# Three products of rounded halves for the projections outside the feed-forwards of a two-block transformer step

## What is computed

```python
def first_block(x, ...):
    h = rms_norm(x, norm_w)
    proj = h @ w_in            # 8200 columns: dn_qkv 1536, dn_z 512, b 4, a 4, swa_q/k/v 3 x 1536, swa_z 512, gates 2048
    qkv = silu(causal_depthwise_conv(dn_qkv, conv_w))
    o_dn = gated_delta_rule_chunked(l2(dq), l2(dk), dv, g, beta)      # chunks of 64, triangular solve
    y_dn = (rms_norm(o_dn, dn_norm_w) * silu(dn_z)) @ w_branch_dn
    ...                        # three dilated windows, 4 heads, rope, softmax over the groups
    y_swa = (o_swa * silu(swa_z)) @ w_branch_swa
    merged = sigmoid(g_dn) * y_dn + sigmoid(g_swa) * y_swa
    return x + merged @ w_out

def second_block(x, mem, ...):
    for l in range(2):
        x = x + 0.5 * swiglu(rms_norm(x, ffn1_norm), ffn1_w_in, ffn1_w_out)     # d_ff 2816
        z = rms_norm(x, mix_norm) @ w_mix_in                                     # 1696 columns
        o = concat(mla(z), swa(z), na(z)) with a norm of each group
        x = x + o @ w_mix_out
        x = x + mem_xattn(rms_norm(x, mem_norm_x), mem, ...)                     # 256 memory tokens, 4 heads of 64
        x = x + 0.5 * swiglu(rms_norm(x, ffn2_norm), ffn2_w_in, ffn2_w_out)
        x = rms_norm(x, block_norm)
    return x
```

## Time and profile before

| | |
|---|---|
| three runs, median (range) | 3507.95 us (3506.88 to 3508.4) |
| the profiled execution | 3507.39 us |
| its span in the profile | 3505.6 us |
| TensorE, matmuls busy | 3214.3 us, 92% |
| VectorE busy | 1275.5 us, 36% |
| ScalarE busy | 905.6 us, 26% |
| mean granted TensorE clock | 0.956 |
| DMA | 235.18 MB, 67 GB/s |

### The profile page before, as it was taken

One profiled execution on the slowest core, in us unless ns is written; L12 is line 12 of the kernel. 1 busy time (PEld: TensorE's weight loads), 2 busy tenths in 40 slices (PEclk: granted clock), 3 DMA queues, 4 the chain that ended last, 5 costly groups with the idle time before them and its releaser, 6 DMA issues. The chain is left out here.

```text
span 3505.6 us, 35266 instructions
## 1 busy us (share of the span) xinstructions
PE 3214.3 (92%) x12500; PEld 2167.7 (62%) x12500; DVE 1275.5 (36%) x1770; ACT 905.6 (26%) x1545; POOL 239.8 (7%) x184
## 2 busy tenths in 40 slices
PE   7978999989989999899989999699998898989997
PEld 3456545454458876364557887588784456468876
DVE  1363124341044432343325442344421535144432
ACT  1211113120023221353323231232211535033321
POOL 0000000000020002000102001300021000120001
PEclk8999899999999999999989999899999999999998
DMA  2200121102212223101012232122222110222221
GB/s 99 71 13 13 42 66 36 54 27 75 78 66 97 98 94 109 35 28 48 31 36 96 96 102 91 49 95 96 96 87 82 36 42 10 63 66 96 97 97 70
DMA packets 68053, 235.18 MB, mean 67 GB/s; under 512 B 10241, under 2 KB 14337, under 8 KB 67201
## 3 DMA queue, kind: packets, MB, share of 16 engines
q1 hardware_dynamic: 65808, 223.93, 19.2%
q10 hardware_dynamic: 2160, 10.15, 0.7%
HBM read 231.95 MB, written 2.10 MB: 67 GB/s over the span
## 5 line engine op out<-in xcount | busy, mean ns | idle before, releaser
L342 PE MATMUL bank<-L_h_hi,L_w_hi 128*128 128x512 f32 x1408 | 557.3, 396 | 53.4 <-DVE L_h_lo L412 38.9
L343 PE MATMUL bank<-L_h_lo,L_w_hi 128*128 128x512 f32 x1408 | 552.5, 392 | 0.0
L344 PE MATMUL bank<-L_h_hi,L_w_lo 128*128 128x512 f32 x1408 | 552.3, 392 | 0.0
L329 ACT CAST L_w_hi<-L_weight_ring 128x1024 fp32r<-128x1024 f32 (+1 forms) x240 | 272.5, 1135 | 879.4 <-PE bank L344 874.4
L335 DVE TENSOR_TENSOR L_w_lo<-L_weight_ring,L_w_hi 128x1024 fp32r<-128x1024 f32 (+1 forms) x240 | 337.9, 1408 | 306.9 <-ACT L_w_hi L329 306.9
L342 PEld LDWEIGHTS bank<-L_h_hi,L_w_hi 128*128 128x128 f32 x1408 | 266.9, 190 | 121.0 <-issue 46.6
L344 PEld LDWEIGHTS bank<-L_h_hi,L_w_lo 128*128 128x128 f32 x1408 | 267.0, 190 | 56.3
L343 PEld LDWEIGHTS bank<-L_h_lo,L_w_hi 128*128 128x128 f32 x1408 | 267.4, 190 | 55.4 <-issue 1.0
L342 PE MATMUL bank<-L_act_hi,L_w_hi 128*128 128x512 f32 x704 | 278.0, 395 | 21.5 <-DVE L_act_lo L479 21.5
L343 PE MATMUL bank<-L_act_lo,L_w_hi 128*128 128x512 f32 x704 | 277.2, 394 | 0.0
L344 PE MATMUL bank<-L_act_hi,L_w_lo 128*128 128x512 f32 x704 | 276.9, 393 | 0.0
(11 more groups left out here) (263 smaller groups left out, 3907.4 us busy)
## 6 DMA issues: line engine op xcount, KB each, us to landing
L_weight_ring<-ffn_in SPq DMA_DIRECT2D x176, 512.0 KB, 3.2
L_weight_ring<-ffn_out SPq DMA_DIRECT2D x64, 704.0 KB, 4.1
B_weight_ring<-w_sqk SPq DMA_DIRECT2D x24, 512.0 KB, 3.2
B_weight_ring<-w_dn SPq DMA_DIRECT2D x16, 512.0 KB, 3.3
B_weight_ring<-w_gate SPq DMA_DIRECT2D x16, 512.0 KB, 3.2
L_weight_ring<-w_sna_qk SPq DMA_DIRECT2D x16, 512.0 KB, 3.3
L_weight_ring<-w_mix_out SPq DMA_DIRECT2D x16, 512.0 KB, 3.2
B_weight_ring<-w_sv SPq DMA_DIRECT2D x12, 512.0 KB, 3.3
```

The lines of the kernel that those rows point to most:

```text
L329: e.copy(hv.w_hi[:, at % 2, 0:width], sh.ring[:, at % RING, 0:width]).then_inc(hv.w_hi_done, 1)
L342: e.matmul(out, w_hi, hi, start=start, stop=False)
L343: e.matmul(out, w_hi, lo, start=False, stop=False)
L344: return e.matmul(out, w_lo, hi, start=False, stop=stop)
```

## The change

Every projection listed above, other than the latent attention's own, the memory's key and value weights, the memory's output and the eight gate-number columns, is computed by three products of halves, as in the feed-forwards. The low half of a strip is now written over the strip in the ring (`ring_lo` is the same memory), the high half has two buffers. The jobs, the convolution loop, the levels, the scan and the merge each get a copy on ScalarE and a subtraction on VectorE for the strip two ahead. The normalized activations become a high and a low tile each: VectorE scales, ScalarE copies, VectorE subtracts.

Around that:

- First block: x is loaded in eight pieces, the first norm waits for the table of ones and the identity alone (`const_load`), and the large tables come later. The gate numbers are computed as an 8-row output over 512 tokens, from the unsplit normalized tile, copied and turned. The low half of h takes the memory of x, and x is loaded again near the end of the block (`x_back`).
- Layers: the banded values are all computed feature-major, then turned; the rotary key's strip is padded to 128 columns; the group outputs are turned through four banks and split in two steps; the memory's key jobs come ahead of its query jobs; where the bias has one segment, bias and maximum are one instruction with a negation after it.

```diff
 def split_strip_dve(e, seen, sh, hv, at, width):
     e.wait_ge(hv.w_hi_done, seen.ready(hv.w_hi_done))
-    e.tensor_tensor(hv.w_lo[:, at % 2, 0:width], sh.ring[:, at % RING, 0:width],
-                    hv.w_hi[:, at % 2, 0:width].bitcast(F32), ALU.subtract).then_inc(hv.w_lo_done, 1)
+    e.tensor_tensor(hv.low(at)[:, 0:width], sh.ring[:, at % RING, 0:width],
+                    hv.high(at)[:, 0:width].bitcast(F32), ALU.subtract).then_inc(hv.w_lo_done, 1)
+def norm_halves_act(e, seen, hv, k):
+    e.wait_ge(hv.h_full, seen.ready(hv.h_full))
+    e.copy(hv.h_hi[:, k, :], hv.full[k % 4]).then_inc(hv.h_hi_done, 1)
+def norm_halves_dve(e, seen, sh, hv, src, gain, k):
+    if k < KT:
+        e.scalar_tensor_tensor(out=hv.full[k % 4], in0=src[:, k, :], scalar=gain[:, k:k + 1],
+                               in1=sh.rstd[:, :], op0=ALU.mult, op1=ALU.mult).then_inc(hv.h_full, 1)
+    if k > 0:
+        e.wait_ge(hv.h_hi_done, seen.ready(hv.h_hi_done))
+        e.tensor_tensor(hv.h_lo[:, k - 1, :], hv.full[(k - 1) % 4], hv.h_hi[:, k - 1, :].bitcast(F32),
+                        ALU.subtract).then_inc(sh.h_done, 1)
...
@@ jobs_pe @@
+                if job.get("halves"):
+                    at = halves_here(e, seen, sh, hv, at, mixed)
+                    for m, (off, (hi, lo)) in enumerate(part):
+                        mm = halves_mm(e, banks[j % 2][:, 0:job["width"]], hv, at - 1, off // P, hi, lo, ...)
@@ jobs_act (after the square), jobs_dve (after the gain, before the rope of the job before) @@
+            if hv is not None:
+                split_strip_act(e, seen, sh, hv, at + j + 2, KT * P)
...
@@ attn_dve @@
+            if len(unit["segs"]) == 1:
+                e.tensor_tensor_reduce(at_.sc[:, u % 2, 0:n], banks[b][:, 0:n], bias, 1.0,
+                                       LOWEST if sink is None else sink[unit["slot"] // TT],
+                                       ALU.add, ALU.max, at_.mx[:, s:s + 1]).then_inc(at_.biased, 1)
+                e.wait_ge(at_.biased, seen.ready(at_.biased))
+                e.tensor_scalar(at_.nm[:, s:s + 1], at_.mx[:, s:s + 1], -1.0, None,
+                                ALU.mult).then_inc(at_.maxed, 1)
...
@@ layer, scalar: before the banded jobs; before the memory jobs @@
+                for i in range(2):
+                    split_strip_act(e, seen, sh, hv, sna_at + i, KT * P)
                 group_norms(0, 1)
...
                 norm_act(e, seen, sh)
-                e.wait_ge(sh.strip_done, seen.ready(sh.strip_done, 2))
+                for k in range(KT):
+                    norm_halves_act(e, seen, hv, k)
+                for i in range(2):
+                    e.wait_ge(sh.strip_done, seen.ready(sh.strip_done))
+                    split_strip_act(e, seen, sh, hv, mem_q_at + i, KT * P)
                 for t in range(2):
                     e.copy(v_mem[:, t, :], banks[t][:, 0:NMEM]).then_inc(v_done, 1)
...
@@ layer, vector: before the banded jobs @@
                     e.memset(qk[DH:P, 2 * i, :], 0.0)
                     x = e.memset(odd_q[0:DH, i, :], 0.0)
                 x.then_inc(padded, 1)
+                for i in range(2):
+                    split_strip_dve(e, seen, sh, hv, sna_at + i, KT * P)
                 scale_groups(0, 1)
...
@@ first block, vector: start; convolutions; levels; merge @@
+                for k in range(KT + 1):
+                    if k < KT:
+                        e.scalar_tensor_tensor(out=h_full[:, k, :], in0=xT[:, k, :], ...).then_inc(sh.h_done, 1)
+                    if k > 0:
+                        e.wait_ge(h_up, k)
+                        e.tensor_tensor(x_lo[:, k - 1, :], h_full[:, k - 1, :], ..., ALU.subtract).then_inc(h_low, 1)
+                    if k in (2, KT):
+                        split_strip_dve(e, seen, sh, hv, 1 + k // KT, KT * P)
...
+                        split_strip_dve(e, seen, sh, hv, 1 + i + 2, KT * P)
...
+                    if 1 <= lv <= 4:
+                        split_strip_dve(e, seen, sh, hv, V_FIRST - 2 + lv - 1, KT * P)
...
+                            split_strip_dve(e, seen, sh, hv, s + 2 + i, KT * P)
                             e.wait_ge(sig_done, seen.ready(sig_done))
@@ first block, tensor: start @@
-                e.wait_ge(loads, 5 * 16)
+                e.wait_ge(const_load, 16)
                 norm_at_once_pe(e, seen, sh)
+                for k in range(KT):
+                    e.wait_ge(sh.h_done, seen.ready(sh.h_done))
+                    mm = e.matmul(banks[5][0:8, :], w[:, k * 8:(k + 1) * 8], h_full[:, k, :], ...)
+                e.wait_ge(ba_copied, 1)
...
+                e.wait_ge(h_low, KT)
```

## The result

The kernel after takes **3382.39 us** (median of 4 runs, 3381.17 to 3384.5) against 3508.03 for the kernel before; the ratio is 0.9643, 95% interval 0.9626 to 0.966. The profiled execution took 3384.5 us, 3382.7 of them span. So 126 us were gained where 167 were forecast, and 3382 lies just outside the range of 3310 to 3380. Apart from the feed-forwards, the parts of the program came out within 4.3 us of their price. What failed is the first term of all, the price of a tile step.

What follows compares the result with a forecast made beforehand. TensorE, busy 3214.3 of 3505.6 us, was taken to bound the kernel. First block -124 and two layers -42 (-21 each) make -166, from 3507.39 to 3341 us; range 3310 to 3380.

Steps and rivals of the forecast that it cites:

- the price of a tile step: All changed projections: a 128x128 by 512 product falls from 0.860 to 0.680 us, gain 0.180 us each.
- Rival 6: Projections miss the feed-forward's price because their halves are laid out otherwise; 96 steps keep 0.86 us: 3358, chance 0.02.
- rivals 1 to 3: VectorE or ScalarE late, 3368, chance 0.15; more cold clock, 3365, 0.10; seams cheaper than read, 3322, 0.13.
- banded attention: Layers: bias and maximum in one instruction, -2 us a layer, between -6 and +6; reduction saved only for units with a sink.
- values: First block: 64 steps gain 11.5 us, two groups hand over banks after one more copy, +2; net -9.5.
- output: First block: 64 steps -11.5 us, shorter cold start -1, longer chain from the merged value +3.7; net -9.
- jobs: First block's query and key jobs: 192 steps -34.5 us, splits delaying the chain before attention +2.6; net -32.
- levels: First block's triangular levels: shorter z pieces gain 2 us, splits ahead of the mask product cost 5; net +3.
- Rival 2: New idles over 5 us at start and seams bring more cold clock, eight places at 3 us: 3365, chance 0.10.
- Rival 1: VectorE or ScalarE late in convolutions (12 us) and norm seams (5 us each): 3368, chance 0.15.
- What would show it: Signs: gates and branches 131 us, 12 jobs 86, convolution strips 5.44 apart, first convolution near 31, seam waits 8 and 14.
- The rule that spoke against the change: Norm scalings with two non-bf16 SBUF sources at half rate, some 1.3 us instead of 0.67: 3361, chance 0.02.

Runs made afterwards that it cites:

- one phase: Padding alone added to the kernel after, so that all halves stand alike modulo 512 bytes in the layers: 3345.87 us, ratio 0.9537.
- five moves: Splits or copies reordered at banded seam, memory seam, job ends, merge end and value copies, against the kernel with one phase; all together 3313.35 us.

## Why the prediction was wrong, and where it was right

Lengths between the same starts of TensorE in the profiled executions, and the change against before in the kernel after, in the one with one phase, and as forecast (us):

| part | before | after | one phase | forecast |
|---|---|---|---|---|
| start to first convolution product | 48.5 | -20.0 | -18.7 | -17 |
| convolution strips | 112.9 | -23.5 | -25.3 | -23 |
| triangular levels | 102.5 | +5.2 | +5.2 | +3 |
| state scan and renorm | 87.3 | -5.9 | -5.9 | -4 |
| values | 60.8 | -5.9 | -6.5 | -9.5 |
| both rows of jobs, to attention | 214.6 | -27.7 | -29.7 | -32 |
| gates and branches | 165.1 | -31.7 | -34.4 | -34.5 |
| output, with the wait before it | 58.2 | -5.4 | -6.1 | -9 |
| whole first block | 1001.1 | -112.1 | -116.9 | -124 |
| layer 1: both feed-forwards | 788.5 | +14.7 | +1.0 | 0 |
| values and latents | 54.2 | -12.3 | -12.0 | -11.5 |
| latent attention and banded jobs | 203.5 | +1.2 | -1.0 | -1 |
| banded attentions | 58.1 | -5.0 | -5.6 | -2 |
| turning and mixer output | 65.4 | -10.7 | -10.9 | -13.5 |
| memory part | 88.7 | +2.7 | +4.0 | +7 |
| whole layer 1 | 1258.4 | -9.4 | -24.5 | -21 |

The table is the first block and layer 1. Layer 2 was 1246.1 us before, from its first feed-forward product to the end of the span; it changed by -1.4 in the kernel after and by -20.0 with one phase. That -1.4 is less than layer 1's -9.4 in part because the kernel before was faster in its second layer (its memory part took 85.4 us there, with the clock at half for 15.5 us, and 88.7 and 21.7 in the first).

- **The step that failed is "The price of a tile step".** It read 0.680 us from the feed-forward of before and carried it to every product, and it took the feed-forward itself as untouched. Both rest on the halves lying as they lay. The change moved them: the low halves went over the ring, in the feed-forward too, and its products are otherwise the same. Measured 0.693; the padding alone gives 36.5 of the missing 41 us back.
- Rival 6 came nearest in kind (the projections don't get the feed-forward's price) but had the wrong cause and 96 steps instead of all 3200. With all halves alike the kernel is 5 us above the forecast, so that is all that rivals 1 to 3 leave in sum. That it is so little is partly luck: start, convolutions, scan, memory part and banded attention gained 2 to 4 us each more than forecast, and values, output, jobs, levels and mixer output 2 to 3 less. Rival 2 is there in part: the idle before values and output grew and took the clock down, 3 us each. Rival 1 isn't: the convolution strips follow each other without a wait.
- **What would show it** was met once the halves stand alike: gates and branches 130.7 us (131 forecast), convolution strips 5.46 apart (5.44), a row of jobs 88.4 (86), the first convolution product at 29.8 (near 31), memory jobs 12.3 us after the reciprocal root (14), first banded product 7.4 us after the last attention matmul (7.7, and the slow clock behind it came too).
- Terms mis-sized: values (+3), output (+3), jobs (+2), levels (+2); the parts of the first block that the table leaves out came to +2.8, +4.5 with one phase, and +2 was forecast. The other way: banded attention (-3 to -4 a layer). The fused instruction is as long as the plain addition where it has no sink (558 ns for 384 columns against 557); with the sink as its starting value it takes 618. But the term counted a gain only for the units with a sink, since in the others a negation takes the reduction's place; the negation is 0.15 us and the reduction was 0.55. Busy times of the kernel after:

```profile
L883 DVE CUSTOM_DVE_ANT_0 L_scores<-bank,L_na_bias 128x384 f32<-128x384 f32 x8 | 4.5, 558 | 6.0 <-PE bank L786 3.8 <-ACT L_probs L843 2.2
L883 DVE DVE_READ_ACCUMULATOR2_ANT L_row_max<- 128x1 f32 x32 | 2.7, 83 | 0.0
L887 DVE TENSOR_SCALAR L_neg_max<-L_row_max 128x1 f32<-128x1 f32 x32 | 4.9, 154 | 1.1
```

  Together 0.80 us a unit of 384 columns without a sink, where an addition of 0.557 and a reduction of 0.553 stood.
- The rule that spoke against the change, half rate for the scalings, didn't decide: a scaling of 512 columns with both large sources in SBUF takes 0.74 us in the memory seam:

```profile
L396 DVE SCALAR_TENSOR_TENSOR L_gained<-residual,L_gains,L_rstd 128x512 f32<-128x512 f32 x4 | 3.0, 744 | 0.0
```

  By the Trainium skill's rule (Vector Engine (DVE) Microarchitecture Reference, "Points that are easy to get wrong") it would be some 1.3, an estimate from the 0.67 us of the earlier trace rows; the measurement decides.

## What to carry to other kernels

A price read from a running stage holds for the placement it was read at: when a change moves, merges or pads tiles, check the unchanged stages too, by counting matmuls over a fixed time at full clock, since busy share stays at 100%. Keep both halves of the weights and the moving values of F32R products at one address modulo 512 bytes a partition; 256 apart did as well in the one run that tried it. Small tables of odd size between large tiles were enough to cost these products 2% of their pace, and the kernel 36.5 us. And when work is moved out of one engine's chain, look at what stands next on that engine: of the five moves here one started TensorE 0.9 us sooner and gave that back at once, because VectorE came later to the next addition. Last, a difference of a few us between two kernels should be looked for in the trace, stretch by stretch: here some of it lay in stretches that the edit didn't touch.

## What the runs showed of the hardware

- Where weights and moving values start in SBUF sets the pace of F32R products of 512 columns. With both halves of the weights alike a matmul takes 226.7 ns at a distance of 0 or 256 bytes, 229 at 64, and 233 at 32 and 128; with the low weights alone elsewhere (the moving values 320 bytes behind them) it takes 231. In the kernel before, plain F32 products took 429 ns a recorded matmul both where the two tiles lie alike modulo 512 (B_hT and the ring) and where they are 320 bytes apart (L_hT and the ring). The Trainium skill (SBUF — State Buffer, section "A bandwidth-pool intuition that's wrong (but worth ruling out)") gives TensorE a second, independent read port for the weights; by that alone the placement should make no difference. The runs here show that it does.
- The clock's fall depends on more than the length of the idle, in the one profiled execution of each kernel. With 3.1 us between two starts in the values it stayed at 1.00 in one kernel and fell to half for 3.4 us in another; in the kernel before it stayed up over 3.3 us, and in the one with one phase it fell over 3.95.
